# A two-layer decoder step on one core: the order at the borders of the feed-forward stages, and the last tiles of layer 0's down projection taken chunk by chunk

## The reference

```
h = RMSNorm(x); z = h @ W_in            # even layer: windowed attention, odd layer: gated chunks
x = x + concat([mixer(z), memattn(z)]) @ W_out
h = RMSNorm(x)
x = x + W_down( silu(causal_dwconv3(h W_g)) * (h W_u) )      # D_FF = 2816
```

## Time and profile before

| what | us |
|---|---|
| three runs | 2143.39, 2143.66, 4429.79 |
| median | 2143.66 |
| the profiled execution | 2143.76 |
| its span, first to last instruction | 2142.0 |
| TensorE busy (matmul) | 2088.6 |
| VectorE busy | 1549.8 |
| GpSimd busy | 1339.1 |
| ScalarE busy | 877.8 |

### The profile page before, as it was taken

One profiled execution on the slowest core, in us unless ns is written; L12 is line 12 of the kernel. 1 busy time (PEld: TensorE's weight loads), 2 busy tenths in 40 slices (PEclk: granted clock), 3 DMA queues, 4 the chain that ended last, 5 costly groups with the idle time before them and its releaser, 6 DMA issues.

```text
span 2142.0 us, 41621 instructions
## 1 busy us (share of the span) xinstructions
PE 2088.6 (98%) x16742; PEld 1988.4 (93%) x16742; DVE 1549.8 (72%) x2154; ACT 877.8 (41%) x1686; POOL 1339.1 (63%) x1221
## 2 busy tenths in 40 slices
PE   9999999999999999899999999999999999989999
PEld 8997679899999999799979996999999999979997
DVE  7456774788888888676765246558888888877675
ACT  6324982543333334444343226344433333344430
POOL 1003644777777877898941223467777778778991
PEclk9999999999999999999999999999999999999999
DMA  5223001122232234444111112102222322354432
GB/s 194 80 107 143 24 6 50 40 86 86 92 114 95 86 121 142 135 147 156 62 42 55 50 37 103 43 30 83 98 85 89 118 95 81 126 180 132 143 99 95
DMA packets 80322, 200.68 MB, mean 94 GB/s; under 512 B 7788, under 2 KB 36452, under 8 KB 76776
## 3 DMA queue, kind: packets, MB, share of 16 engines
q1 hardware_dynamic: 77304, 189.16, 25.8%
q10 hardware_dynamic: 2832, 8.94, 1.1%
HBM read 153.63 MB, written 46.48 MB: 93 GB/s over the span
## 4 chain that ended last, share of the span: by engine, by line
PE 80%; DVE 9%; issue 4%; POOL 3%; ACT 3%; DMA 0%; SPq 0%; DVEq 0%; ACTq 0%; POOLq 0%
PE ps L1526 16%; PE ps L1528 16%; PE ps L1527 16%; PE ps L1042 8%; PE ps L1044 8%; PE ps L1043 8%; PE ps L1616 3%; POOL w_lo L813 2%; DVE a_buf L2693 2%; DVE t_buf L2757 1%; DVE a_buf L2688 1%; PE ps L1442 1%; ACT s_exp L1906 1%; PE ps L1397 1%; POOL w_sum L835 1%
## 5 line engine op out<-in xcount | busy, mean ns | idle before, releaser
L1526 PE MATMUL ps<-t_hi,w_hi 128*128 128x264 f32 x1408 | 403.9, 287 | 7.1 <-DVE t_lo L2647 3.7
L1528 PE MATMUL ps<-t_hi,w_lo 128*128 128x264 f32 x1408 | 400.4, 284 | 0.0
L1527 PE MATMUL ps<-t_lo,w_hi 128*128 128x264 f32 x1408 | 400.0, 284 | 0.0
L1686 ACT ACTIVATE w_hi<-raw 128x512 fp32r<-128x512 f32 (+2 forms) x304 | 184.5, 609 | 426.2 <-PE ps L1044 292.3
L813 POOL TENSOR_TENSOR w_lo<-raw,w_hi 128x512 fp32r<-128x512 f32 (+1 forms) x252 | 300.1, 1199 | 81.7 <-ACT w_hi L1686 81.1
L1526 PE MATMUL ps<-g_hi,w_hi 128*128 128x264 f32 x1120 | 322.1, 288 | 20.5 <-DVE g_lo L2660 12.0
L1042 PE MATMUL ps<-h_hi,w_hi 128*128 128x352 f32 x1008 | 332.2, 330 | 6.6 <-DVE h_lo L2276 6.4
L1044 PE MATMUL ps<-h_hi,w_lo 128*128 128x352 f32 x1008 | 325.2, 323 | 0.0
L1043 PE MATMUL ps<-h_lo,w_hi 128*128 128x352 f32 x1008 | 325.0, 322 | 0.0
L1527 PE MATMUL ps<-g_lo,w_hi 128*128 128x264 f32 x1120 | 322.3, 288 | 0.0
L1528 PE MATMUL ps<-g_hi,w_lo 128*128 128x264 f32 x1120 | 322.2, 288 | 0.0
(11 more groups left out here) (282 smaller groups left out, 4896.0 us busy)
## 6 DMA issues: line engine op xcount, KB each, us to landing
raw<-in_w SPq DMA_DIRECT2D x141, 512.0 KB, 3.2
g_f<-g_spill SPq DMA_DIRECT2D x70, 528.0 KB, 5.0
g_spill<-c_buf SPq DMA_DIRECT2D x20, 1056.0 KB, 4.0
raw<-in_w SPq DMA_DIRECT2D x82, 256.0 KB, 3.2
g_spill<-t_buf SPq DMA_DIRECT2D x20, 792.0 KB, 6.5
s_mk<-in_s_mk SPq DMA_DIRECT2D x2, 2048.0 KB, 9.8
s_mv<-in_s_mv SPq DMA_DIRECT2D x2, 2048.0 KB, 14.3
out_y<-x ACTq DMA_DIRECT2D x7, 528.0 KB
```

The source lines that it names most:

```text
L1526: pe.matmul(out, hi_w[:, k, :], hi_x[:, k, t0:t0 + HC], start=begin, stop=False, skip_group_check=True)
L1527: pe.matmul(out, hi_w[:, k, :], lo_x[:, k, t0:t0 + HC], start=False, stop=False, skip_group_check=True)
L1528: mm = pe.matmul(out, lo_w[:, k, :], hi_x[:, k, t0:t0 + HC], start=False, stop=end, skip_group_check=True)
L1686: return act.activation(out, in_, ACT.Copy)
```

## The change

It has six parts. The order of layer 0's last tiles becomes chunk by chunk (q % 8, q // 8) on all engines, with the cut of h at every tile and the ring of squares counted accordingly. The sums of even down pairs move from `t_buf` to `rb`, and the third pair's first sum waits for `c_scaled`. In the down stage `high_weights` goes behind `high_g`. In a gate pair `norm_second(n, 0)` goes behind `plus(2, ...)`. The third norm sum and its root go behind product 5. The high and low part of T2's parts 0 to 2 go ahead of the scaling of the last half.

```diff
+def last_tile(layer, q):
+    return (q % KD, q // KD) if layer == 0 else (q // NCH, q % NCH)
+def ring_chunk(w, p):
+    return p // (KD - 1) if w == 2 else p % NCH
...
-        sums_even = t_buf[:, :, :].rearrange("p s n -> p (s n)")
+        sums_even = rb[:, :]
...
 def add_squares
-                    c = p % NCH
-                    pool.wait_ge(squared, (N_SSQ + NCH) * (w - 1) + NCH + p + 1)
-                    if p >= NCH:
+                    c = ring_chunk(w, p)
+                    pool.wait_ge(squared, (N_SSQ + NCH) * (w - 1) + (c if w == 2 else NCH - 1) + p + 2)
+                    if w == 2 and p % (KD - 1) > 0:
+                        pool.wait_ge(ssq_added, adds_before(w) + p)
+                    if w != 2 and p >= NCH:
                         pool.wait_ge(ssq_added, adds_before(w) + p - 2)
 def sum_block
                 if pair == NPAIR + 2:
-                    pool.wait_ge(up_scaled, 3 * NG * (l + 1))
+                    pool.wait_ge(c_scaled, NF * (l + 1))
 TensorE gate_up
-                        if n == 0 and pos == 4:
+                        if n == 0 and pos == 5:
                             pe.wait_ge(rooted, NCH * (w - 1) + 2)
                             norm_mean(w, 2)
 TensorE last_down, VectorE add_last
-                    oo, c = q // NCH, q % NCH
+                    oo, c = last_tile(l, q)
 ScalarE square
-                oo, c = e // NCH, e % NCH
+                oo, c = last_tile(0, e) if w == 2 else (e // NCH, e % NCH)
-                    p = e - NCH
+                    p = e - c - 1 if w == 2 else e - NCH
 ScalarE early_operands
+                if oo == KD - 1:
+                    act.wait_ge(proj, 3 * ((R_OUTA, R_OUTB)[l] + OUT_U))
+                    act.wait_ge(operand_sum, sum_at(l, "T2", 2))
+                    scopy(t2_hi[:, 0:3, :], t2_f[:, 0:3, :]).then_inc(operand_cut, 1)
 ScalarE ffn
-                act.wait_ge(operand_sum, sum_at(l, "T2", 2))
-                scopy(t2_hi[:, 0:3, :], t2_f[:, 0:3, :]).then_inc(operand_cut, 1)
-                        if n == 0 and pos == 4:
+                        if n == 0 and pos == 5:
                             norm_root_of(w, 2)
-                        high_weights(l, j + 8)
                         if p == 0 and pos < 3:
                             high_g(l, 0, 4 + pos)
                         if g + 1 < NGRP and (q, pos) in G_AT:
                             high_g(l, g + 1, G_AT.index((q, pos)))
+                        high_weights(l, j + 8)
 ScalarE, layer 0's last tiles
                         act.wait_ge(std_added, e + 1)
-                        if e % NCH == 0:
-                            high_of_h(2, e // NCH)
+                        high_of_h(2, e)
                         square(2, e)
                     high_up(O_INB + 1, R_INB + 1)
-                    for e in range(KD, KD * NCH):
-                        high_of_h(2, e)
 VectorE early_operands
+                    if oo == KD - 1:
+                        dve.wait_ge(operand_cut, cut_at(l, "T2", 0))
+                        dve.wait_ge(operand_sum, sum_at(l, "T4", 2))
+                        TT(t2_lo[:, 0:3, :], t2_f[:, 0:3, :], t2_hi[:, 0:3, :].bitcast(F32), ALU.subtract) \
+                            .then_inc(operand_low, 1)
                     dve.wait_ge(halves_scaled, 2 * HK * l + k + 1)
 VectorE low_t2
-                dve.wait_ge(operand_cut, cut_at(l, "T2", 0))
-                TT(t2_lo[:, 0:3, :], t2_f[:, 0:3, :], t2_hi[:, 0:3, :].bitcast(F32), ALU.subtract).then_inc(operand_low, 1)
 VectorE gate_pair
-                        parts_taken(n, 3)
-                        norm_second(n, 0)
...
                     plus(2, a_buf[:, 1, second])
                     if i > 0:
                         parts_taken(n, 4)
+                        norm_second(n, 0)
                         norm_second(n, 1)
 VectorE, the last tiles
                     add_last(q)
-                    if l == 0 and q % NCH == 2:
-                        low_of_h(2, q // NCH)
+                    if l == 0 and q > 0:
+                        low_of_h(2, q - 1)
                 if l == 0:
-                    for e in range(KD, KD * NCH):
-                        low_of_h(2, e)
+                    low_of_h(2, KD * NCH - 1)
```

## The result

The changed kernel takes 2118.24 us (median of five runs, 2118.08 to 2119.49) against 2143.66 us. The ratio of the medians is 0.9881, its 95% interval 0.9868 to 0.9895. The forecast was 2118.6 us, "within 2%". The profiled execution took 2118.24 us, its span is 2116.5 us.

What follows compares the result with a forecast made beforehand. TensorE, busy for 98% of the span, was taken as the bound, so only its pauses and their slow matmuls could pay. Terms 5.9 + 0.7 + 13.2 + 5.9 - 0.5 = 25.2 us gave 2118.6 us, range 2109 to 2127.

Steps and rivals of the forecast that it cites:

- Scaling behind reading: Gate pairs, product 6: VectorE reads before it scales, removing 0.31 us 19 times; gain 5.9 us.
- g ahead of weights: Down stage's long g wait: g comes 0.31 us earlier on ScalarE; 0.35 us per layer, together 0.7 us.
- Sums in the space of 1/rms: Third down pair: GpSimd's sums start 6.3 us earlier, so the x wait and its slow matmuls go; gain 13.2 us.
- 40 slow matmuls: Behind the x waits of both layers: 40 matmuls at the lower clock go, 0.1 us each, within the 13.2 us.
- Last tiles chunk by chunk: Layer 0's last tiles: h_lo wait and slow matmuls go, 6.4 us, less 0.5 us of stall; net 5.9 us.
- The border: T2 ahead and third norm sum one product later: T2 starts unchanged, norm wait moves to later waits; sum -0.5 us.
- (a): Border pays too: VectorE and GpSimd alternate differently and TensorE's pace decides; 9.9 us more gain, 2108.7 us; chance 0.12.
- (d): Down stage: the long g wait shrinks by its larger part, 9 us; 2109.6 us; chance 0.04.
- (b): Layer 0's last tiles stretch to 1.65 us each on VectorE; up to 3 us more, 2121.6 us; chance 0.10.
- (c): Third down pair: x wait is replaced, sums stay late; half of 13.2 us stays, 2125.2 us; chance 0.06.
- (e): Layer 0's last tiles lock in series at 3.2 us each; 48 us more, 2167 us; chance 0.02.
- (f): Sums' new wait never frees anything, VectorE holds them elsewhere; 13.2 us less gain, 2131.8 us; chance 0.03.

Runs made afterwards that it cites:

- the kernel before with the one late edit: Kernel before the change, with only the cut of a weight block put behind the cut of g in the down stage: 2138.58 us.
- two different cures: On the changed kernel, g's blocks 4 to 6 cut ahead of the second pair's first weight block: 2116.30 us; or 36 unneeded matmuls filling the g wait: 2116.98 us.

## Why the prediction was right, and where not

The total is right to 0.4 us, but not each term of it; that it is so close is in part luck, as the terms show.

- **Scaling behind reading**, forecast 5.9 us. The stages show 6.6 and the undo run 6.4. Right; the gap costs 0.33 us instead of 0.31.
- **g ahead of weights**, forecast 0.7 us. The step that failed is "Per layer 0 to 0.75 us; I take 0.35": it is 0 at the g wait. ScalarE's cut came earlier as forecast, but VectorE's low part of g lasted 1.84 us behind GpSimd instead of 1.54 (it starts at 865.55, TensorE at 868.11), so both orders reach the product 11.6 us behind the start of the stage. What I did not see at all is that the same edit shortens the x wait by 1.35 us a layer when it stands alone, since a g cut stands between the late sums and VectorE.
- **Sums in the space of 1/rms**, forecast 13.2 us. In that stretch the change gained 11.3, and the undo run says 9.8 for this part. The mechanism was right: the sums start without a stand (5.4 us earlier in the stage, forecast 6.3), and the x wait with its slow matmuls is gone. Mis-sized is "40 slow matmuls", which took the stretch behind the g wait as fixed: it grew from 14 and 15 matmuls to 26 and 18, 15 x 0.1 = 1.5 us. 2.8 of the 11.3 us could have been had from the other edit alone.
- **Last tiles chunk by chunk**, 6.4 us less 0.5 of stall. It brought 6.46 us and no stall at all; the undo run gives 5.5 us, where its slow stretch is 9 matmuls instead of 17. "VectorE loses about 0.3 us a tile" was right (1.44 us a tile against 1.18), but TensorE's lead was enough: 0.26 x 18 less 2 is 2.7 us, under the 4.2 us that the prediction gives it, and so were its own 3 to 4 us. The 24 tiles take 28.13 us, below the 28.4 to 30 named as a sign. The Trainium skill's rule on the port (SBUF — State Buffer, section "SBUF: two separate sides") would have made the stall larger, not smaller. The trace agrees that the two engines hold each other up and shows that it was not the bound here. At the 1.58 us a tile that the prediction names for it, its own way of counting (0.4 x 18, less 2 and 4.2) gives 1.0 us of stall and not 1.5. The timelines have a low part of VectorE's against GpSimd's adding, and one while GpSimd stands:

```profile
1083.04 0.93 POOL L814 TENSOR_TENSOR ssq<-ssq,sq_ring 128x352 f32<-128x352 f32 x1 [0.71 <-ACT sq_ring L1730]
1083.06 1.29 DVE L2287 SCALAR_TENSOR_TENSOR h_lo<-x,gain,h_hi 128x352 fp32r<-128x352 f32 x1
1084.27 0.51 DVE L2899 TENSOR_TENSOR x<-x,ps 128x352 f32<-128x352 f32 x1
1084.70 0.57 DVE L2287 SCALAR_TENSOR_TENSOR h_lo<-x,gain,h_hi 128x352 fp32r<-128x352 f32 x1
```

- **The border**, forecast -0.5 us; -0.6 in the stages. The sum came out, its steps only in part. T2 was to start when it did, and starts 0.5 us later in the border (its wait is 2.9 us, now for w_lo). The rb wait goes and a wait in front of the first up pair takes its place, as forecast, but at product 0 and not at product 3. And the layers came the other way round: 0.17 us for layer 0 where I had 0.4 to 1.4, 0.43 for layer 1 where I had 0.1. Layer 0's reciprocals do begin 1.35 us later, but the work behind them, which I took as fixed, is 1.18 us shorter, since the two scalings no longer meet GpSimd. That is rival (a)'s other alternation; it only made good what the delay cost. That -0.6 came out beside -0.5 is luck.
- **Untouched stages** gave 1.8 us (1.4 at the start of the program, 0.4 in layer 1's mixer), which is in no term. They made up for what the sums fell short, by luck. The start differs by as much between runs of one order (B11 at 394.95 to 396.10 us in the other kernels, whose fronts are all the same, and at 395.62 us in the kernel before with the one late edit), so it is spread, not gain.

Of the rivals, (d) asked whether the long g wait would shrink by 9 us: it did not, and the runs say more: with the wait gone by another order of ScalarE's cuts, the whole program gains 1.9 us. (a), (b), (c), (e) and (f) did not come.

## What to carry to other kernels

Where a fuller engine stands behind a wait, removing the wait buys only the difference: two different cures of one 4.5 us wait, in three runs, ended at 212.4 to 212.55 us, and only less work on GpSimd went below. Look at the busy share of every engine over the next few stages, not over the whole span (GpSimd has 63% of the span and 96% of this stretch), before you price a wait. That busy share can hold time in which two engines lengthen each other. And two edits that reach for one wait don't add: undoing each in turn gives 9.8 and 0 us of the 11.3 here, and doing one alone (2.8 us) shows the overlap.

## What the runs showed of the hardware that I had not expected

- The stretch at the lower clock behind a pause is not a fixed price. Behind the same 4.5 us g wait of layer 0 it was 13 to 27 matmuls in ten profiled runs, and behind the same 2.9 us T2 wait it was none, 13 to 16, or 24. The runs differ in nothing near by. 0 to 24 there is worth up to 2.3 us, more than the distance of seven of the twelve runs here from the changed kernel.
- Behind the g wait it goes entirely when TensorE is given work that nobody needs: granted clock 1.00 in both windows, at no cost to the product that waits (it starts 11.27 us behind the start of the stage instead of 11.62).
- VectorE and GpSimd lengthen each other to more than twice: GpSimd's 128x256 low part takes 0.73 us alone and up to 1.83 us in turns with VectorE, and VectorE's 128x352 low part 0.57 and 1.29 us. A write of zeros of the same size took 0.31 us beside the same work of VectorE's.
- A pause need not be long to cost more than itself: behind 0.33 us instead of 0.12 between two starts the first matmul lasts 0.39 instead of 0.28 us, 19 times in each run that has the gap, and the granted clock around it reads 1.00.
